# Half of three adaLN sums moved from TensorE to VectorE

## What is computed

```
c_act = silu(c)
ada   = c_act @ w_ada + b_ada                    # 1024 -> 6 x 1024
sh_a, sc_a, g_a, sh_f, sc_f, g_f = split(ada, 6)
h     = rmsnorm(x, norm_mix_w) * (1 + sc_a) + sh_a
proj  = h @ w_in                                 # 1024 -> 9232
# gated linear attention and HGRN2 on parts of proj, merged,
# then w_out, a ConvFFN (w_up, causal conv, w_down) and a last rmsnorm
```

## Time and profile before

| what | value |
|---|---|
| median of three runs | 957.17 us |
| profiled execution | 954.61 us |
| its span | 952.6 us |
| TensorE busy | 921.8 us, 97% |
| VectorE busy | 524.7 us, 55% |
| ScalarE busy | 466.0 us, 49% |
| GpSimd busy | 164.2 us, 17% |
| first slot starts | 24.04 us |
| last slots of k = 6 end | 51.6 us |

### The profile page before, as it was taken

How to read it: one execution, slowest core, us unless ns; L and a number is a source line. 1 busy time by engine, 2 the same in 40 slices (tenths; PEclk the granted TensorE clock), 3 DMA queues, 4 the chain that set the end, 5 groups by cost and what they waited for, 6 DMA issues and landing times.

```text
span 952.6 us, 13844 instructions
## 1 busy us (share of the span) xinstructions
PE 921.8 (97%) x4980; PEld 758.9 (80%) x4980; DVE 524.7 (55%) x677; ACT 466.0 (49%) x632; POOL 164.2 (17%) x110
## 2 busy tenths in 40 slices
PE   4999999999999999999999897999999999999997
PEld 4778887888878888788888776888888888888885
DVE  3547952578434785338753666655445454643327
ACT  5556845458445575436654553533333333523324
POOL 2001421114221123211150300112211112100000
PEclk9999999999999999999999999999999999999999
DMA  9938233282232822246231351342333332243202
GB/s 327 371 92 265 86 89 111 70 240 67 67 117 82 238 59 78 68 131 191 74 108 44 107 158 44 89 133 88 92 106 88 104 94 91 86 135 108 88 1 89
DMA packets 145362, 111.43 MB, mean 117 GB/s; under 512 B 3409, under 2 KB 136800, under 8 KB 145072
## 3 DMA queue, kind: packets, MB, share of 16 engines
q1 hardware_dynamic: 144816, 110.64, 38.1%
q0 software_dynamic: 160, 0.20, 0.1%
q10 hardware_dynamic: 351, 0.14, 0.1%
HBM read 106.77 MB, written 4.19 MB: 116 GB/s over the span
## 4 chain that ended last, share of the span: by engine, by line
PE 93%; ACT 3%; DVE 2%; issue 1%; ACTq 0%; DVEq 0%
PE ps L1195 28%; PE ps L1197 27%; PE ps L1196 27%; PE ps L1325 2%; PE ps L1310 2%; PE ps L1321 2%; PE ps L1229 1%; PE ps L1335 1%; PE ps L1297 1%; DVE w_lo L813 1%; PE ps L1283 1%; ACT L620 1%; ACT w_hi L510 0%; ACTq L524 0%; PE ps L1343 0%
## 5 line engine op out<-in xcount | busy, mean ns | idle before, releaser
L1195 PE MATMUL ps<-h_hi,w_hi 128*128 128x512 f32 x864 | 344.7, 399 | 6.9 <-DVE h_lo L1112 3.3
L1197 PE MATMUL ps<-h_hi,w_lo 128*128 128x512 f32 x864 | 337.4, 390 | 0.0
L1196 PE MATMUL ps<-h_lo,w_hi 128*128 128x512 f32 x864 | 337.1, 390 | 0.0
L813 DVE TENSOR_TENSOR w_lo<-raw,w_hi 128x1024 fp32r<-128x1024 f32 x142 | 190.3, 1346 | 89.5 <-ACT w_hi L510 88.8
L1195 PEld LDWEIGHTS ps<-h_hi,w_hi 128*128 128x128 f32 x864 | 162.6, 188 | 44.9 <-issue 10.2
L1196 PEld LDWEIGHTS ps<-h_lo,w_hi 128*128 128x128 f32 x864 | 162.8, 188 | 34.5 <-issue 2.1
L1197 PEld LDWEIGHTS ps<-h_hi,w_lo 128*128 128x128 f32 x864 | 162.7, 188 | 34.1
L510 ACT ACTIVATE w_hi<-raw 128x1024 fp32r<-128x1024 f32 x142 | 148.4, 1052 | 70.2 <-PE ps L1197 48.8
L1195 PE MATMUL ps<-w_hi,h_hi 128*128 128x512 f32 x296 | 117.6, 397 | 6.5 <-DVE h_lo L853 3.8
L1197 PE MATMUL ps<-w_hi,h_lo 128*128 128x512 f32 x296 | 115.4, 390 | 0.0
L1196 PE MATMUL ps<-w_lo,h_hi 128*128 128x512 f32 x296 | 115.4, 390 | 0.0
(11 more groups left out here) (197 smaller groups left out, 918.7 us busy)
## 6 DMA issues: line engine op xcount, KB each, us to landing
raw<-in_w_in_dram SPq DMA_DIRECT2D x68, 512.0 KB, 4.2
raw<-in_w_up_dram SPq DMA_DIRECT2D x44, 512.0 KB, 3.8
ada_w<-in_w_ada_dram SPq DMA_DIRECT2D x32, 512.0 KB, 4.6
raw<-in_w_down_dram SPq DMA_DIRECT2D x22, 512.0 KB, 3.3
ada_w<-in_w_ada_dram SPq DMA_DIRECT2D x8, 1024.0 KB, 9.4
raw<-in_w_out_dram SPq DMA_DIRECT2D x8, 512.0 KB, 3.6
x_tok<-in_x_dram SPq DMA_DIRECT2D x4, 512.0 KB, 4.9
w_first<-in_w_in_dram SPq DMA_DIRECT2D x8, 256.0 KB, 7.6
```

What stands on the lines that cost most here:

```text
L813: dve.tensor_tensor(w_lo[:, slot(u)].rearrange("p k c -> p (k c)"), raw[:, raw_slot(u)].rearrange("p k c -> p (k c)"), w_hi[:, slot(u)].re ...
L1195: pe.matmul(dst, a_hi, b_hi, start=start and i == 0, stop=False)
L1196: pe.matmul(dst, a_hi, b_lo, start=False, stop=False)
L1197: last = pe.matmul(dst, a_lo, b_hi, start=False, stop=stop and i == n - 1)
```

## The change

For pieces 1 to 3 TensorE multiplies the channel blocks 0 to 3 alone, 16 matmuls in place of 32. Blocks 4 to 7 are accumulated by VectorE in `ada0_half(i)`: one multiplication and three multiply-adds of 128x512 elements into a part of `x_tok`, each waiting for the one before it. TensorE then adds that tile over the partitions with four more matmuls, whose weights are 32 columns of ones, into the same bank. It waits for VectorE's fourth operation (`ada0_part`) ahead of them. On VectorE, `ada0_half(i)` stands behind `h_rest(2i-1)` and ahead of `ada0_finish(i)`. Piece 0 is unchanged.

The tables move as well: the sums of pieces 1, 2 and 3 go from behind the slots (0,0), (1,2), (3,2) to behind (0,3), (2,0), (4,0), and the turns from behind (0,1), (1,3), (3,3) to behind (1,0), (2,1), (4,1).

```diff
--- before.py
+++ after.py
@@ -75,8 +75,8 @@
 
 
 PIECES = KT // 2
-SUMS_AFTER = {(0, 0): 1, (1, 2): 2, (3, 2): 3}
-TURN_AFTER = {(0, 1): 1, (1, 3): 2, (3, 3): 3}
+SUMS_AFTER = {(0, 3): 1, (2, 0): 2, (4, 0): 3}
+TURN_AFTER = {(1, 0): 1, (2, 1): 2, (4, 1): 3}
 
 
 def slot(u):
@@ -241,6 +241,7 @@
         lr_done = sem("lr_done")
         lr_taken = sem("lr_taken")
         ada0_summed = sem("ada0_summed")
+        ada0_part = sem("ada0_part")
         ada0_row_made = sem("ada0_row_made")
         ada0_turned = sem("ada0_turned")
         ada0_made = sem("ada0_made")
@@ -893,10 +894,27 @@
             x_scaled(0)
             x_scaled(1)
             first_lo(0)
+            def ada0_half(i):
+
+                dve.wait_ge(ada0_in[i], 32)
+                dve.wait_ge(x_turned, 2)
+                dve.wait_ge(ada0_summed, i)
+                part = x_tok[:, 0, 0:T].rearrange("p (a c) -> p a c", a=2)
+                for n in range(4):
+                    k = KT // 2 + n
+                    if n == 0:
+                        ins = dve.tensor_scalar(part, ada_w0[:, i % 2, k], c_act[:, k:k + 1], None, ALU.mult)
+                    else:
+                        dve.wait_ge(ada0_part, 4 * (i - 1) + n)
+                        ins = dve.scalar_tensor_tensor(out=part, in0=ada_w0[:, i % 2, k], scalar=c_act[:, k:k + 1],
+                                                       in1=part, op0=ALU.mult, op1=ALU.add)
+                    ins.then_inc(ada0_part, 1)
+
             for k in range(KT):
                 h_rest(k)
                 if k in (1, 3, 5):
                     i = k // 2 + 1
+                    ada0_half(i)
                     ada0_finish(i)
                     x_scaled(2 * i)
                     x_scaled(2 * i + 1)
@@ -1224,11 +1242,16 @@
 
                 pe.wait_ge(ada0_in[i], 32)
                 pe.wait_ge(ada0_row_made, i)
-                for k in range(KT):
+                for k in range(KT if i == 0 else KT // 2):
                     for j in range(4):
                         last = pe.matmul(ps[32 * j:32 * j + 32, 7, 0:P], c_rep[:, k],
                                          ada_w0[:, i % 2, k, j // 2, (j % 2) * P:(j % 2 + 1) * P],
-                                         start=k == 0, stop=k == KT - 1)
+                                         start=k == 0, stop=i == 0 and k == KT - 1)
+                if i:
+                    pe.wait_ge(ada0_part, 4 * i)
+                    for j in range(4):
+                        last = pe.matmul(ps[32 * j:32 * j + 32, 7, 0:P], ones[:, 0:32], x_tok[:, 0, j * P:(j + 1) * P],
+                                         start=False, stop=True)
                 last.then_inc(ada0_summed, 1)
 
             def ada0_turn(i):
```

## The result

The changed kernel takes 958.03 us in the median of 22 runs (955.86 to 960.23), the kernel before 956.82 beside it. The ratio is 1.0024, 95% interval 1.0015 to 1.0033: slower by 0.24%, 2.3 us (1.4 to 3.2). The medians alone differ by 1.2 us: the runs of before fall into two groups, ten from 953.4 to 955.4 and twelve from 956.8 to 957.7, and their median lies at the lower edge of the upper one. Twelve more runs of the changed kernel gave 1.0021 (1.0004 to 1.0038) against the runs of before beside them. The forecast was +3.1 us.

The account below looks back on a forecast made before the run. TensorE, busy 97% of the span, was taken to bound the kernel. Waits of 4.65 us plus about 0.6 for restarts and first slots, less 2.1 of work, gave +3.1 on 957.17: 960.3 us, range 957.4 to 963.6.

Parts of the forecast that it names:

- TensorE's work: Sums of pieces 1 to 3 on TensorE: each falls from 1.88 to 1.18 us, 2.1 us less for three.
- VectorE's chain: Four added VectorE operations per halved piece: 2.8 us together, range 2.6 to 3.1.
- The waits: TensorE: 1.7 us for `h_lo` ahead of (2,0), then 1.5 and 1.45 inside the sums of pieces 2 and 3.
- Starting again: TensorE's four added matmuls behind a wait: 0.24 us and some 0.2 for starting again.
- The slow stretch costs slots what it cost sums: Slow stretch at the first slots: about 0.43 us a matmul instead of 0.23, the same 1.6 us cost, no gain.
- The time of 960.3: Whole kernel: the median of before, 957.17 us, plus 3.1; range 957.4 to 963.6.
- The slowed clock: Rival: new TensorE waits bring on slow stretches; one gives +4.7 us (961.9), two +6.3 (963.5); chance 0.22.
- The expectation for the clock at 1.00 from 28.2 us on: TensorE's granted clock was to be at 1.00 from 28.2 us on, a sign listed for the forecast.
- The load of piece 3: Load issued at about 29.85 us instead of 28.54, landed by 39, needed at 43.6: no effect.

Follow-up runs that it names:

- order alone: The kernel before with only the two tables of the change; all 32 matmuls of each sum stay on TensorE. Ratio to before 1.0030, 2.9 us.
- changed (second): The changed kernel run again word for word, for a second profile. Ratio to the kernel before 1.0021 (1.0004 to 1.0038).
- piece 3 alone: The changed kernel with only piece 3 halved, pieces 1 and 2 as before. 953.58 us, ratio to before 0.9985.
- before (both): The kernel before, unchanged, in its first and a second profile; first slot to low-rank matmuls took 27.53 and 27.98 us.
- halving alone: The changed kernel with the tables of before; TensorE waits 2.7 us in piece 2. Ratio to before 1.0034, 3.3 us.
- chain cut: The changed kernel with two of VectorE's four operations left out, blocks 6 and 7 missing from the sums. Ratio to before 0.9999.
- quarter: The changed kernel with only blocks 6 and 7 on VectorE, 24 + 4 matmuls on TensorE. Ratio to before 1.0031, 3.0 us.
- pieces 1 and 3 (first): The changed kernel with only pieces 1 and 3 halved, sums behind (0,1), (1,2), (4,0). Ratio to before 1.0003.
- piece 1 earlier: The changed kernel with piece 1's sums behind (0,1) and turn behind (0,2), two slots earlier. Ratio to before 1.0033.
- piece 1 alone: The changed kernel with only piece 1 halved, its sums behind (0,1); pieces 2 and 3 summed as before. Ratio to before 1.0004.
- pieces 1 and 3 (again): The version with only pieces 1 and 3 halved, sums behind (0,1), (1,2), (4,0), run again for a second profile. Ratio to before 1.0008.
- pieces 1 and 3, piece 1 at its old place: The changed kernel with only pieces 1 and 3 halved, piece 1's sums behind (0,0) and turn behind (0,1). Ratio to before 1.0017.

## Why the prediction was right

- **TensorE's work.** 1.18 us a piece were forecast, 1.23 measured. Right.
- **VectorE's chain.** 2.8 us forecast; 0.41 and three times 0.79 with the handoffs are 2.8. Right.
- **The waits.** 1.7, 1.5 and 1.45 us forecast, 1.70, 1.40 and 1.28 measured, at the three places named. From the turn of piece 1 to the slot (2,0) 3.75 us were forecast, 3.78 measured (33.04 to 36.82). The order alone kept the first and had no other; cutting VectorE's chain took away the two others.
- **Starting again.** 0.24 + 0.2 us for the four matmuls behind a wait: 0.43 measured.
- **The slow stretch costs slots what it cost sums.** A matmul of a slot took 0.43 us in it, as forecast (26.53 to 29.52 in the first profile). The second profile of the changed kernel shows it directly: its slow stretch lasts from 25.4 to 28.8 us, 3.4 us as in before and wholly in the stage, and the stage takes 30.66 us, 3.1 more than 27.53. The L1278 behind k = 6 starts 30.73 us behind the first slot, where 54.7 less 24.04 is 30.66. In the first profile the stage is 3.0 us longer at equal clock (28.9 against 25.9). So the 3.1 us stand in the stage. The whole time gave 2.3 and 2.0 us, with intervals up to 3.2 and 3.6.
- **The time of 960.3.** Measured 958.03, 2.3 us less and only 0.6 above the lower end of the range. The median of before beside it was 956.82 instead of 957.17, which is 0.35 us of it; 1.1 lie between the 2.3 us of the ratio and the 1.2 by which the medians differ; 0.8 is the ratio's 2.3 us against 3.1. I cannot say whether these 0.8 us are given back or are noise of the clock. That the absolute time fell inside the range owes as much to the width of the range as to the sum; it is the waits that bear the forecast out.
- **The slowed clock.** Named as a rival for this kernel. Its profiles show no slow stretch behind the new waits: from 31 us on (29 in the second) the granted clock is 1.00 up to the end of the stage and beyond. The version with a single wait of 2.7 us shows exactly this rival.
- **The expectation for the clock at 1.00 from 28.2 us on** was wrong: the slow stretch of the first profile lasted from 23.3 to 30.2 us, 6.8 us instead of 3.4. I had taken its place and length for a property of the kernel.
- **The load of piece 3.** Issued at 32.09 us, 2.2 later than forecast, since the first slot came 1.7 us later and the slow stretch covered more of the slots. The queue did run dry, 0 GB/s near 33 us, and nothing waited for it.

## What to carry to other kernels

An engine at 97% busy can still stand inside a loop through other engines. Before work is taken from it, add up that loop once per round, handoffs included, and compare it with the busy engine's work in the same round: here 8.55 us of latency against 7.0 us of work, and in the first round 5.0. Split a round's work only where the helper is idle and its result comes in before the busy engine asks for it, and measure an effect of 0.2% at equal clock in the stage it belongs to, besides the whole time. Then look for where the clock was low, far behind the stage too: a slow stretch of 3.4 us, hundreds of microseconds later, costs some 1.5 us here, more than the 1 us gained in the stage.

## What the runs showed of the hardware

- Identical instructions ahead of the change put the first slot anywhere from 23.9 to 26.7 us, and identical ones behind the stage took 899.5 to 903.8 us, over 14 profiles. The second is settled by two waits that all 14 profiles have. In before the first of them reads

```profile
527.81 0.47 PE L1195 MATMUL ps<-h_hi,w_hi 128*128 128x512 f32 x1 [2.57 <-DVE h_lo L1066]
```

It lasts 2.56 or 2.57 us everywhere, the second, near 587 us, 3.33. What differs is how long the granted clock is 0.50 at their end or behind them:

| profiles | near 530 us | near 587 us | from the end of the stage to the end of the span |
|---|---|---|---|
| changed (second), piece 3 alone | none | none | 899.5, 899.7 |
| before (both), changed (first), halving alone, chain cut | none | 3.4 us | 901.0 to 901.1 |
| quarter, pieces 1 and 3 (first) | 3.4 us | none | 901.2, 901.1 |
| order alone, piece 1 earlier, piece 1 alone, pieces 1 and 3 (again) | 3.4 us | 3.4 us | 902.6 to 903.0 |
| pieces 1 and 3, piece 1 at its old place | 3.4 us | 6.8 us | 903.8 |

A slow stretch of 3.4 us behind the stage so costs some 1.5 us.
- TensorE's records can be slow while the granted clock reads 1.00. In the changed kernel the eight records at L1265 took 2.08 us and the sums of piece 0 2.46; in the second profile of it 1.16 and 1.88, the second as in the earlier trace rows at full clock:

```profile
16.68 2.08 PE ps L1265 x8
18.76 2.46 PE ps L1247 x64
```

```profile
17.00:18.00 1.00, 1.00 (x6) 1.00 (x6) 0.89 (x7) 0.00 (x0) 0.00 (x0) 1.00 1.08 384
```

- An idle time of 2.7 us between busy stretches had 6.8 us at 0.50 at its end and behind it; waits of 1.7 and 1.4 us, 2 us apart, had none. The wait of 2.57 us near 530 us had a slow stretch in 7 of 14 profiles, the one of 3.33 us in 10 of 14. The Trainium skill, TensorE: Matmul & The Clock Gate, Part 1, says that the clock is set by how busy the engine has been recently. The trace agrees in so far as each slow stretch between 20 and 900 us stands at the end of idle time or behind it; but the length of that idle time alone does not decide, since the same wait had it in one profile and not in the next.
- Seven versions ran at a lower mean clock (0.9895 to 0.9912) than before beside them (0.9920 to 0.9931): the order alone, the halving alone, the quarter, piece 1 earlier, and the three that halve piece 1 but not piece 2. The changed kernel (0.9931, 0.9922), its cut chain (0.9928) and halving piece 3 alone (0.9929) did not. Of the seven, the halving alone has the slow stretch at its wait of 2.7 us. The other six all have the one near 530 us, in seven profiles of seven, and none of the versions at the usual clock has it, in six profiles. It lowers the mean clock by 0.0018 (half of 3.4 us on 955 us), where their runs lack 0.0012 to 0.0036. So a shift in the first 55 us went together with another clock 475 us later. With one or two profiles of each version that is a pattern and not a proof, and why the same wait has a slow stretch in these versions alone stays open.
- As a rough estimate, the mean of time times granted clock over all runs, less that of before beside them, gives +1.9 us for the changed kernel (second batch), +1.9 for the order alone, +1.8 for piece 1 earlier, +1.7 for the halving alone, +1.5 for the quarter, +0.7 for the cut chain, -1.0 for piece 1 alone, -1.5 and -1.6 for pieces 1 and 3, -1.9 for these with piece 1 at its old place and -1.7 for piece 3 alone, each good to about 1 us. It shares the limit of the second point, that a stretch can be slow while the clock reads 1.00. But apart from the cut chain the signs are those of the stage: with the clock taken out, the versions without a new wait over 0.7 us beat the kernel before.
